# Two mixer layers of a six-layer chain: the stick-breaking mask moves into the scores, its sums into the softmax loop, and VectorE scales the softmax weights

## The reference, cut to what matters

```python
# stick-breaking, 4 heads; z = q k^T * scale; strict: key position < query position
log_beta = jax.nn.log_sigmoid(z)
log_1mb = jnp.where(strict, jax.nn.log_sigmoid(-z), 0.0)
tail = lax.cumsum(log_1mb, axis=3, reverse=True) - log_1mb
a = jnp.where(strict, jnp.exp(log_beta + tail), 0.0)
o_sb = a @ v
# one layer
heads = rms_norm(jnp.stack([o_moba, o_mla, o_sb], axis=2), head_out_g[l])
mixed = jnp.concatenate([heads.reshape(bsz, seq, 3 * GROUP_WIDTH), o_ssm], axis=-1)
x = x + jnp.einsum("bsc,cd->bsd", mixed, w_out[l])
```

## Time and profile before

| what | value |
|---|---|
| median of 3 runs | 2330.27 us (2327.37 to 2339.81) |
| the profiled execution | 2331.76 us, span 2330.1 us |
| PE busy, mean granted clock | 95%, 0.972 |
| DVE, ACT, POOL busy | 66%, 38%, 17% |
| first layer in question: first softmax score to out product | 1674.44 to 1725.78 us |
| second layer: first softmax score | 2053.24 us |

### The profile page before, as it was taken

One profiled execution on the slowest core, in us unless ns is written; L12 is line 12 of the kernel. 1 busy time (PEld: TensorE's weight loads), 2 busy tenths in 40 slices (PEclk: granted clock), 3 DMA queues, 4 the chain that ended last, 5 costly groups with the idle time before them and its releaser, 6 DMA issues.

```text
span 2330.1 us, 33338 instructions
## 1 busy us (share of the span) xinstructions
PE 2213.6 (95%) x13185; PEld 1915.0 (82%) x13185; DVE 1527.5 (66%) x1923; ACT 873.9 (38%) x1160; POOL 407.5 (17%) x227
## 2 busy tenths in 40 slices
PE   7999999999999999999899999989889999978999
PEld 7988788898788788788798978869568997847998
DVE  7854744797754668645785285466567887367886
ACT  3344444331344322444314444432554333354332
POOL 6632000160000050000262300005120002330000
PEclk9999999999999999999999999999889999979999
DMA  7510565552565443655451056545115554403552
GB/s 213 176 37 25 193 190 189 167 186 64 167 193 182 160 161 97 199 187 174 145 181 55 1 173 194 183 145 165 51 51 173 190 182 134 154 6 114 190 188 91
DMA packets 265597, 333.67 MB, mean 143 GB/s; under 512 B 16492, under 2 KB 228593, under 8 KB 265473
## 3 DMA queue, kind: packets, MB, share of 16 engines
q1 hardware_dynamic: 265473, 331.93, 44.5%
HBM read 330.84 MB, written 1.05 MB: 142 GB/s over the span
## 4 chain that ended last, share of the span: by engine, by line
PE 85%; DVE 9%; ACT 3%; issue 2%; POOL 1%; DVEq 0%; POOLq 0%; ACTq 0%
PE bank L541 42%; PE bank L513 27%; PE bank L952 2%; PE bank L881 2%; PE bank L585 1%; PE bank L1009 1%; DVE w_hi L1931 1%; PE bank L575 1%; PE bank L732 1%; PE bank L940 1%; ACT w_hi L1459 1%; ACT mats L1413 1%; ACT xh L1413 1%; DVE w_lo L1933 1%; PE bank L838 1%
## 5 line engine op out<-in xcount | busy, mean ns | idle before, releaser
L1933 DVE TENSOR_TENSOR w_lo<-ring,w_hi 128x2048 fp32r<-128x2048 f32 (+3 forms) x297 | 561.9, 1893 | 328.5 <-ACT w_hi L1459 325.3
L1459 ACT ACTIVATE w_hi<-ring 128x2048 fp32r<-128x2048 f32 x204 | 385.5, 1890 | 463.2 <-PE bank L541 298.8
L1373 POOL TENSOR_TENSOR w_lo<-ring,w_hi 128x1536 fp32r<-128x1536 f32 (+3 forms) x71 | 277.1, 3903 | 1436.2 <-DVE w_hi L1931 1436.2
L541 PE MATMUL bank<-w_lo,xh 128*128 128x512 f32 x992 | 268.9, 393 | 1.5 <-POOL w_lo L1373 1.4
L541 PE MATMUL bank<-w_hi,xh 128*128 128x512 f32 x928 | 250.9, 392 | 10.6 <-ACT xh L1413 6.8
L513 PE MATMUL bank<-xh,w_lo 128*128 128x256 f32 (+2 forms) x1880 | 246.2, 284 | 5.0 <-POOL w_lo L1373 5.0
L541 PE MATMUL bank<-w_hi,xl 128*128 128x512 f32 x928 | 249.0, 390 | 0.0
L513 PE MATMUL bank<-xh,w_hi 128*128 128x256 f32 (+1 forms) x1816 | 242.7, 287 | 2.3 <-DVE w_hi L1931 2.3
L513 PEld LDWEIGHTS bank<-xh,w_lo 128*128 128x128 f32 (+2 forms) x1880 | 232.2, 188 | 8.0 <-issue 5.7
L513 PEld LDWEIGHTS bank<-xh,w_hi 128*128 128x128 f32 (+1 forms) x1816 | 229.9, 192 | 9.2 <-issue 5.5
L513 PE MATMUL bank<-xl,w_hi 128*128 128x256 f32 (+1 forms) x1816 | 237.2, 283 | 0.0
(11 more groups left out here) (310 smaller groups left out, 2605.6 us busy)
## 6 DMA issues: line engine op xcount, KB each, us to landing
ring<-in_ffn_w_in_dram SPq DMA_DIRECT2D x264, 512.0 KB, 4.5
ring<-in_ffn_w_down_dram SPq DMA_DIRECT2D x88, 512.0 KB, 4.3
ring<-in_gdn_w_in_dram SPq DMA_DIRECT2D x64, 512.0 KB, 5.2
ring<-in_ffn_w_out_dram SPq DMA_DIRECT2D x44, 512.0 KB, 4.2
ring<-in_w_in_dram SPq DMA_DIRECT2D x36, 512.0 KB, 4.6
ring<-in_hgrn_w_in_dram SPq DMA_DIRECT2D x32, 512.0 KB, 4.8
ring<-in_gla_w_in_dram SPq DMA_DIRECT2D x24, 512.0 KB, 4.2
ring<-in_gdn_w_out_dram SPq DMA_DIRECT2D x16, 512.0 KB, 4.0
```

The lines of the kernel that those rows point to most:

```text
L541: m = nc.tensor.matmul(bank[:, 0:width], xin[:, k0 + k, rows_of], w[:, k, c * width:(c + 1) * width], start=(first and step == 0 and k == ...
L1373: g.tensor_tensor(w_lo[:, unit % RING, part], ring[:, unit % RING, part], high_part(unit)[:, part], ALU.subtract).then_inc(*pool_lo.tick())
L1459: nc.scalar.activation(high_part(u)[:, 0:n], ring[:, u % RING, 0:n], ACT.Copy).then_inc(*act_hi.tick())
L1933: v.tensor_tensor(w_lo[:, u % RING, 0:share], w[:, 0:share], high[:, 0:share], ALU.subtract).then_inc(*dve_lo.tick())
```

## The change

VectorE adds the strict mask (now 0 and -1e30, no longer 1 and 0) while it scales the scores z. The masked places then give 0 in log(1 - beta) and in the weights, and GpSimd's twelve operations a layer fall away; `sb_l1` holds -log(1 - beta), which VectorE computes, and the tail is subtracted. Tail sums 0 to 2 are issued behind the transposes of softmax 2, 4 and 6. VectorE scales the softmax weights in place of ScalarE. The exponentials of the stick-breaking weights write `at2` at once, the first three within the loop. The copies of the value products are gone: squares and norms read the PSUM banks. ScalarE casts each normalised group behind the next group's factor, VectorE's split of a weight unit stands behind the gated output, and the filler in front of the out product is gone in these two layers.

```diff
                 for n in range(8 + 3):
                     if n == 3:
                         stay_awake(FILL["softmax"])
@@ -1120,26 +1130,20 @@
                     if n >= 3:
                         n -= 3
                         b = psum.claim(pe, "probs", layer, n)
-                        pe.wait_ge(*act_four.at("probs", layer, n))
+                        pe.wait_ge(*dve_four.at("normalised", layer, n))
...
-                for h in range(4):
-                    b = psum.claim(pe, "tail", layer, h)
-                    pe.wait_ge(*pool_four.at("log1mb", layer, h))
...
+                        if n in (2, 4, 6):
+                            tail(n // 2 - 1)
+                tail(3)
 
...
-                    pe.wait_ge(*(act_four if m < 2 else pool_four if m == 2 else dve_four).at("causal", layer, m))
+                    pe.wait_ge(*(act_four if m < 3 else dve_four).at("causal", layer, m))
...
                     four(layer)
-                    stay_awake(FILL["mixed"])
                     out_project(layer)
...
-                keep(strict[:, c:c + HALF], [[1, HALF]], -1, -1)
+                keep(strict[:, c:c + HALF], [[1, HALF]], -1, -1, fill_=-1e30)
...
-                for h in range(4):
-                    pool.wait_ge(*dve_four.at("log beta", layer, h))
-                    l1 = sb_l1[:, h, :]
-                    g.tensor_tensor(l1, sb_t[:, h, :], at2[:, h, :], ALU.subtract).then_inc(*pool_four.tick())
-                    pool.wait_ge(*pool_four.now())
-                    g.tensor_tensor(l1, l1, strict[:, :], ALU.mult).then_inc(*pool_four.tick("log1mb", layer, h))
-                for h in range(4):
-                    pool.wait_ge(*act_four.at("a", layer, h))
-                    g.tensor_tensor(at2[:, h, :], sb_t[:, h, :], strict[:, :], ALU.mult).then_inc(*pool_four.tick("causal", layer, 2))
...
                 act.wait_ge(*dve_four.at("causal", layer, 3))
+                def weights(h):
+                    act.wait_ge(*dve_four.at("log a", layer, h))
+                    run(s, at2[:, h, :], sb_t[:, h, :], ACT.Exp, "causal", layer, 2)
+
...
-                    if 2 <= n < 8 + 2:
-
-                        p = prob(n - 2)
-                        act.wait_ge(*dve_four.at("inverse sum", layer, n - 2))
-                        run(s, p[:, 0:HALF], p[:, 0:HALF], ACT.Copy, scale=small[:, n - 2, 2:3])
-                        run(s, p[:, HALF:TRI], p[:, HALF:TRI], ACT.Copy, "probs", layer, n - 2, scale=small[:, n - 2, 3:4])
+                    if n in (7, 9, 11):
+                        weights(n // 2 - 3)
...
-                for h in range(4):
-                    act.wait_ge(*dve_four.at("log a", layer, h))
-                    run(s, sb_t[:, h, :], sb_t[:, h, :], ACT.Exp, "a", layer, h)
-                act.wait_ge(*pool_four.at("causal", layer, 2))
-                for m in (0, 1, 3, 2):
+                weights(3)
+                act.wait_ge(*s.now())
+                order = (0, 1, 3, 2)
+                for m in order:
                     if m < 3:
                         act.wait_ge(*pe_four.at("o", layer, m))
-                        b = psum.bank("o", layer, m)
-                        run(s, oc4[:, m, :], b[:, :], ACT.Copy, "o", layer, m)
-                        run(s, two(sq, m), b[:, :], ACT.Square, "o2", layer, m)
-                        psum.release(s, "o", layer, m)
+                        run(s, two(sq, m), psum.bank("o", layer, m)[:, :], ACT.Square, "o2", layer, m)
                     else:
                         act.wait_ge(*dve_four.at("gated", layer))
                         run(s, two(sq, 3), oc4[:, 3, :], ACT.Square, "o2", layer, 3)
...
+                for n, m in enumerate(order):
                     act.wait_ge(*pe_four.at("o2", layer, m))
                     w, sc = (2 * T, 1.0 / 64) if m < 3 else (T, 1.0 / 256)
                     rstd(s, stat[:, m, 0:w], psum.bank("o2", layer, m)[:, 0:w], ("o2", layer, m), sc, C_RMS_EPS,
                          "rstd", layer, m)
-                for m in (0, 1, 3, 2):
-                    act.wait_ge(*dve_four.at("mixed", layer, m))
-                    run(s, two(xh, m), two(y, m), ACT.Copy, "mixed hi", layer, m)
+                    if n:
+                        high(order[n - 1])
+                high(order[3])
...
-                    ts(s, at2[:, h, :], b[:, 0:TRI], 0.125, ALU.mult, None, None, "z", layer, h)
+                    stt(s, at2[:, h, :], b[:, 0:TRI], 0.125, strict[:, :], ALU.mult, ALU.add, "z", layer, h)
...
+                def log_weights(h):
+                    dve.wait_ge(*s.at("log beta", layer, h))
+                    dve.wait_ge(*pe_four.at("tail", layer, h))
+                    tt(s, sb_t[:, h, :], sb_t[:, h, :], psum.bank("tail", layer, h)[:, 0:TRI], ALU.subtract, "log a", layer, h)
+                    psum.release(s, "tail", layer, h)
+
                 for n in range(8 + 2):
+                    if n in (6, 8):
+                        log_weights(n // 2 - 3)
...
-                        v.reciprocal(small[:, n, 2:4], small[:, n, 2:4]).then_inc(*s.tick("inverse sum", layer, n))
+                        v.reciprocal(small[:, n, 2:4], small[:, n, 2:4]).then_inc(*s.tick())
+                        p = prob(n)
+                        dve.wait_ge(*s.now())
+                        ts(s, p[:, 0:HALF], p[:, 0:HALF], small[:, n, 2:3], ALU.mult)
+                        ts(s, p[:, HALF:TRI], p[:, HALF:TRI], small[:, n, 3:4], ALU.mult, None, None, "normalised", layer, n)
                         if n % 2:
                             h = n // 2
                             dve.wait_ge(*act_four.at("log1p z", layer, h))
+                            stt(s, sb_l1[:, h, :], at2[:, h, :], 0.0, sb_t[:, h, :], ALU.max, ALU.add, "log1mb", layer, h)
                             stt(s, sb_t[:, h, :], at2[:, h, :], 0.0, sb_t[:, h, :], ALU.min, ALU.subtract, "log beta", layer, h)
-                for h in range(4):
-                    dve.wait_ge(*pe_four.at("tail", layer, h))
-                    tt(s, sb_t[:, h, :], sb_t[:, h, :], psum.bank("tail", layer, h)[:, 0:TRI], ALU.add, "log a", layer, h)
-                    psum.release(s, "tail", layer, h)
-                split()
+                log_weights(2)
+                log_weights(3)
...
-                dve.wait_ge(*s.now())
-                for m in (0, 1, 3, 2):
+                split()
+                order = (0, 1, 3, 2)
+                for n, m in enumerate(order):
                     dve.wait_ge(*act_four.at("rstd", layer, m))
+                    o = oc4[:, 3, :] if m == 3 else psum.bank("o", layer, m)[:, :]
                     for j in range(2):
                         g = PT_MISC * P + (R_HEADG + 6 * l + 2 * m if m < 3 else R_SSMG + 2 * l) + j
                         r = stat[:, m, j * T:(j + 1) * T] if m < 3 else stat[:, 3, 0:T]
-                        stt(s, y[:, 2 * m + j, :], oc4[:, m, j * T:(j + 1) * T], par(g), r, ALU.mult, ALU.mult, "mixed", layer, m)
-                mixed_low(layer, s, act_four, (0, 1, 3, 2))
+                        stt(s, y[:, 2 * m + j, :], o[:, j * T:(j + 1) * T], par(g), r, ALU.mult, ALU.mult, "mixed", layer, m)
+                    if m < 3:
+                        psum.release(s, "o", layer, m)
+                    if n:
+                        mixed_low(layer, s, act_four, order[n - 1:n])
+                mixed_low(layer, s, act_four, order[3:])
                 split(HI - 1)
```

25 lines of the change are left out of this document (15 added, 10 removed).

## The result

The changed kernel takes 2314.29 us (median of 15 runs, 2312.93 to 2330.4), the kernel before 2331.41 (15 runs, 2323.47 to 2344.2). The ratio is 0.9933, 95% interval 0.9915 to 0.9951. So the change is worth 15.6 us by the ratio (11.4 to 19.8) and 17.1 by the medians: a small effect of 0.7%, whose interval leaves out 1.

What follows compares the result with a forecast made beforehand. Bound taken as a half-clock chain over all engines, first scores to out product, in the last two mixers. 5.0 - 2.4 = 2.6 us a layer, 5.2 in all, from the 2330.27 median gave 2325, range 2317 to 2332.

Steps and rivals of the forecast that it cites:

- head start: Last two mixers: the out product of each layer starts earlier, taken as 5.0 us a layer.
- cold out product: Out product without filler: TensorE idles about 4 us, the clock falls to half, costing 2.4 us a layer.
- Where does the clock rise?: TensorE around the value products: full clock expected from 1706.2 to 1707.9, each microsecond of it worth half a microsecond.
- first laying out: Softmax loop to out product, layer 4, step by step: out product at 1720.1 instead of 1725.78, 5.7 us earlier.
- the clock rises early, too: Rival, softmax loop: denser TensorE work raises the clock before 1707.9, saving 7.5 us a layer, 2315; chance 8%.
- Chain of the loop: Softmax loop: earlier transposes, tail sums between them; first value product at 1707.6, 3.2 us earlier than before.
- Scalings: VectorE's two softmax scalings: 0.65 us a pair with the wait for the reciprocal.
- Value products to out product: Behind the loop: masks and copies gone, casts reordered; from first value product at 1707.6 to out product at 1720.1.
- By that rule the filler is worth its place: Ahead of the out product: the skill's rule on idle gaps speaks against removing the 18 filler passes.
- the clock holds: Rival: TensorE's clock stays full across the gap ahead of the out product, 2 x 5.0 gained, 2320; chance 20%.
- slower: Rival: half clock at the out product costs 3.2 us a layer and outweighs the head start, 2332; chance 12%.
- the change doesn't do what it says: Rival, softmax loop: transposes wait for VectorE instead, out product only 2.4 earlier, clock takes it back, 2330; chance 10%.

Runs made afterwards that it cites:

- e1_same: The changed kernel with no edit, timed and profiled again: 2318.14 us, ratio 0.9945 against the kernel before.
- e4: The kernel before without the 18 filler passes ahead of the two out products: 2333.55 us, ratio 1.0003.
- e5: The changed kernel with the softmax weights scaled by ScalarE again: 2331.13 us, ratio 1.0008.
- e8: The kernel before with one part of the change alone, VectorE scaling the softmax weights: 2324.04 us, ratio 0.9969.
- e3: The changed kernel with the four tail sums, their log weights and weights behind the softmax loop again: 2322.29 us, ratio 0.9968.
- e2: The changed kernel with the 18 filler passes ahead of the out product put back: 2316.63 us, ratio 0.9953.
- e11: The changed kernel with the norms' part undone (copies, all factors before casts, split ahead of the gated part): 2316.89 us, ratio 0.9944.
- e12: The changed kernel with GpSimd making log(1 - beta) for three of four heads: 2313.87 us, ratio 0.9928.
- e13: The changed kernel with a short filler of 8 passes ahead of the out product: 2321.46 us, ratio 0.9947.
- e7: The kernel before with filler matmuls in the softmax loop, nothing else edited: 2328.8 us, ratio 0.9997.
- e6: The changed kernel with filler matmuls in TensorE's idle places of the softmax loop: 2315.29 us, ratio 0.9944.
- e10: The changed kernel with ScalarE scaling the softmax weights again, plus loop fillers: 2320.89 us, ratio 0.9964.
- e14: The changed kernel with GpSimd's log(1 - beta) for three heads, loop fillers and the short 8-pass filler: 2311.9 us, ratio 0.9921.

## Why the prediction was wrong

I predicted 5.0 us of head start a layer less 2.4 for a cold out product. Measured in e1_same: head starts of 8.5 and 8.2 us, less 2.0 and 1.5 given back behind the out product, so 6.6 and 6.7.

The step that failed is the question "Where does the clock rise?". I took the whole second half of the loop at half clock, to 1707.9 as before, and priced two transposes and two tail sums there at half clock (0.65 + 1.6 + 0.65 + 1.6 = 4.5 us). They took 2.54 (2085.42 to 2087.96), since the clock had risen at about 2077.3, 20 us behind the first score and not 33.5. Those 2.0 us and 0.6 of an earlier arrival make the loop 5.8 rather than 3.2 shorter. The rest of the 4.1 us a layer between 2.6 and 6.7 is 0.7 that I had gone below my own first laying out (5.7, taken as 5.0 after a second one of 4.4), and 0.4 to 0.9 by which the cold out product cost less than 2.4.

What TensorE did ahead of that rise I had laid out myself: scores 4 and 5 and transposes 1 from 2072.30, then transposes 2 at 2075.97 and tail sum 0 with hardly a break, where before 2.70 us of waiting for ScalarE stood ahead of transposes 2. I had this as a rival ("the clock rises early, too", 7.5 a layer, 8%) and put it low because 4.09 us of work in 1695 to 1700 had not raised the clock. That row bears on the old order alone, in which waits of 2.7 us stand on both sides of that work. The measured 6.6 a layer lies between my forecast and that rival, nearer the rival, whose 7.5 left out the cold out product.

That the order brings the clock up, and not luck of one run, is seen by counting loops. With ScalarE's scaling (before, e4, e5) all 6 are at half clock for 24 us or more. With VectorE's scaling and late tails (e8, e3) it is 17 to 20 us in all 4. With both (changed, e1, e2, e11, e12, e13) it is 10 us in 10 of 12 and 24 or more in the other 2.

Point by point:

- Chain of the loop: right. Transposes 2 came 18.6 us behind the first score (predicted 1692.9 - 1674.44 = 18.5), score 6 at 20.5 (20.8), VectorE had it at 22.0 (22.4), transposes 4 at 24.0 (24.2), transposes 6 at 28.1 (28.7). At full clock on both sides the order gains 3.2 (e7 against e6), the very number of the sum; that is luck in part, since mine was laid out at half clock.
- Scalings: 0.286 and 0.347 us, and 0.65 from one reciprocal to the next (2084.53 to 2085.18): as taken. The Trainium skill, "VectorE: DVE Perf Modes", section "Mode 2×_2P — use both read ports for one tensor", is borne out by the rows above: 128 columns more cost 61 ns in the scaling (286 to 347) and 122 in the reduce (287 to 409).
- Value products to out product: predicted 12.5 (1707.6 to 1720.1), measured 12.20. Last square to out product 5.23 (5.3).
- The other term of the sum, the cold out product: 3.09 us idle (I said 4.2), 3.4 us at half clock in the first 10 (I said 3 to 5), a cost of 1.5 to 2.0 (I said 2.4). Right in kind. The clock is no certainty there either: of 18 out products without filler in nine profiles of the changed kernel and its variants, 5 were at full clock in their first 10 us.
- "By that rule the filler is worth its place": half true. It keeps the clock (e2), but at 18 passes it holds up the product by what it saves. The rule of the Trainium skill, "TensorE: Matmul & The Clock Gate", section "HAM oscillation — how this bites in real kernels", agrees with the half clock seen behind the gap of 3.09 us; the time did not follow.
- The rivals "the clock holds", "slower" and "the change doesn't do what it says": out. The clock did not hold in either layer of the two profiles of the changed kernel, and the other two don't fit loops that are 5.8 us shorter.

Why did the scaling matter most? e5 takes it back and loses 14.2 us over both layers by its loops (75.4 against 61.2), all of the gain. 2.5 a layer is the wait itself (e10 against e6). The other 4.8 goes with the clock (e5 against e10): with TensorE's work in pieces it stays down or falls again. The two can't be added as independent terms: a filled loop without the new order gains 2.7 at best (e7, first layer), and in the new order filling gains 0.05 (e6).

The last piece is the size: 13.3 us are explained by stretches, 15.6 measured (11.4 to 19.8). The difference is within what the runs can tell.

## What to carry to other kernels

When an edit removes a wait in a chain that stands at half clock, price it twice, at half and at full clock, and give the second case a real chance: closing the waits brought the clock up early in 10 of 12 loops here. Then ask which engine paces the stretch; where TensorE waits for another engine anyway, half clock cost nothing here (0.05 us in e6), and fillers brought nothing. Ask again once that engine is relieved (0.5 us in e14 against e12). A filler ahead of a dependent product must find its PSUM bank free and end no later than the operands arrive; read both from the trace and cut it to length.
